# Transposes of an expert chunk three matmuls later, behind the wait for the next chunk's second weight unit

## The chip, the cores and the metric

The kernel runs on one core of one Trainium2 chip. The metric is device time in microseconds. Before the change the median of three runs is 1539.44 us (1539.42 to 1541.25).

## The reference

One step of a small hybrid decoder, for 256 prompt tokens and 32 sample tokens that share all weights: a convolution block, a dense SwiGLU, shared keys and values, windowed attention, and at the end a mixture of eight SwiGLU experts of which each token takes two. Everything is float32. The change lies in the mixture alone:

```python
h = rms_norm(x, g); hf = h.reshape(-1, D_MODEL)               # D_MODEL 1024
top_v, top_i = lax.top_k((hf @ w_router), TOP_K)              # 2 of 8
gates = jax.nn.softmax(top_v, axis=-1)
for e in range(N_EXPERTS):                                    # D_FF_EXPERT 3584
    he = jax.nn.silu(hf @ w_eg[e]) * (hf @ w_eu[e])
    y = y + combine[:, e:e + 1] * (he @ w_ed[e])
```

## The kernel before

Tokens are routed first: each of eight trips of the expert loop gathers the tokens of one expert into 128 slots. A trip walks through 14 chunks of 256 hidden columns. A chunk needs three weight units of 128 x 2048 float32 (1 MB each): two for gate and up together (each holds half of the 1024 input rows, four blocks of 512 columns), one for the down product.

Float32 products are made of three products of a shorter format. Each unit lands in one of six buffers (`land`). ScalarE casts it (`w_hi` or `d_hi`), VectorE subtracts the cast from the original (`w_lo` or `d_lo`), and TensorE runs three matmuls for each block of weights (`mm3`, lines 385 to 387): high by high, low by high, high by low. So a unit has twelve matmuls of 512 columns, and the down product twelve as well. The `w` pair has four buffers (two chunks), `d` has two.

The engines walk through a trip in orders written out by hand, with semaphores between them:

- TensorE, for chunk `ch`: `gate_up(ch+1, 0)`, the first unit of the next chunk; `turn(ch)`, two transposes of `he` of this chunk into bank 6; `gate_up(ch+1, 1)`, the second unit; `down(ch)`. A `gate_up` waits first for `split`, the count of finished `w_lo`. `turn` waits for `he_ready`, and `down` for `heT_ready` and `d_split`. In the last chunk of a trip, `gate_up` belongs to the next trip and stands in conditional blocks. Behind some chunks other work follows: matmuls that place the next trip's slots (line 744), transposes of the next trip's gathered tokens (line 738), and in the last trip sums that come back (line 770).
- ScalarE: `silu(ch)` when both units of the chunk are multiplied; the cast `d_hi` of chunk `ch+1`, which waits until `down(ch-1)` has freed its buffer; `heT_hi` (line 1189), which waits for the transposes; then both casts `w_hi` of chunk `ch+2` (line 1114).
- VectorE: `he` (line 1634), the product of SiLU and up half; `d_lo` of chunk `ch+1` (line 1628); in chunk 4 also the next trip's picks (`place`, line 1588); `heT_lo` (line 1660); then both `w_lo` of chunk `ch+2` (line 1527), each of which counts `split` up.
- SyncE issues the loads of the units in order, each when the buffer's last user, a `w_lo` or `d_lo`, is done.

Ahead of the loop stand the two units of the first chunk. The transposes use line 806.

Of the kernel before, what the change touches and what calls it, by code (L numbers as in the profile page):

```python
# [39 lines left out]
P = 128  # L40
# [17 lines left out]
NCH = FE // CH  # L58
# [55 lines left out]
def build(nc, io):  # L114
    with ExitStack() as ctx:
# [3 lines left out]
        def sem(name):  # L119
            return ctx.enter_context(nc.semaphore(name))  # L120

        bank = [ctx.enter_context(nc.psum_tensor(f"bank{i}", [P, 512], F32)) for i in range(8)]
# [79 lines left out]
        def c(name):  # L202
            return con[:, CON[name][0]:CON[name][1]]

        ident = c("ident")
# [50 lines left out]
        esilu_ready, he_ready, heT_done, heT_hi_ready, heT_ready = (  # L256
            sem(n) for n in ("esilu_ready", "he_ready", "heT_done", "heT_hi_ready", "heT_ready"))
# [124 lines left out]
        def _(pe):  # L382
            def mm3(out, w, x, start, stop):

                pe.matmul(out, w[0], x[0], start=start, stop=False)  # L385
                pe.matmul(out, w[0], x[1], start=False, stop=False)  # L386
                return pe.matmul(out, w[1], x[0], start=False, stop=stop)  # L387

            def wblock(n, i):
                a, b = i * P, (i + 1) * P  # L390
                return w_hi[n % RING][:, a:b], w_lo[n % RING][:, a:b]

            def H(k, a=0, b=T):
                return H_hi[:, k, a:b], H_lo[:, k, a:b]

            def G(k):
                return G_hi[:, k, :], G_lo[:, k, :]
# [49 lines left out]
            for j in range(KT_D):  # L447
# [3 lines left out]
                for half in range(2):  # L451
                    out = bank[2 * (j % 2) + half][:, 0:T]
                    for k in range(KT_D):
                        if j == 0 and half == 0:
                            wait_h(0, k)
                        last = mm3(out, wblock(U_PW1 + j, KT_D * half + k), H(k), k == 0, k == KT_D - 1)
# [11 lines left out]
            for k in by_end:  # L468
# [4 lines left out]
                last = pe.matmul(MEAN[:, 0:T], c("mean_d"), C[:, k, :], start=(k == by_end[0]), stop=(k == by_end[-1]))  # L473
# [4 lines left out]
            for d in range(KT_D):  # L478
# [4 lines left out]
                for k in range(KT_D):  # L483
                    if d == 0:
                        wait_h(1, k)
                    last = mm3(bank[d % 4][:, 0:T], wblock(n, KT_D * (d % 2) + k), H(k), k == 0, k == KT_D - 1)
                last.then_inc(pw2_done, 1)

            for half in range(2):
                for i in range(FH):  # L490
# [5 lines left out]
                    for part in range(2):  # L496
# [3 lines left out]
                        for k in range(KT_D):  # L500
                            if f == 0 and part == 0:
                                wait_h(2, k)
                            last = mm3(out, wblock(n, KT_D * part + k), G(k), k == 0, k == KT_D - 1)
# [3 lines left out]
                for d in range(KT_D):  # L507
                    if KT_D * half + d >= 2:
                        pe.wait_ge(x_ffn, KT_D * half + d - 1)
                    for i in range(FH):  # L510
# [6 lines left out]
                        last = mm3(bank[4 + d % 2][:, 0:T], wblock(n, blk), (A_hi[:, a, :], A_lo[:, a, :]),  # L517
                                   i == 0, i == FH - 1)
# [5 lines left out]
            for t in range(2):  # L524
                for k in range(KT_D):
                    if t == 0:
                        wait_h(3, k)
                    last = mm3(bank[t][:, 0:T], wblock(U_K, KT_D * t + k), H(k), k == 0, k == KT_D - 1)
# [13 lines left out]
            for i, (t0, nt) in enumerate(TT):  # L542
                for k in range(KT_D):
                    a = k * 256
                    last = mm3(bank[2 + i // 2][0:nt, 256 * (i % 2):256 * (i % 2) + 256],
                               H(k, t0, t0 + nt), (w_hi[U_V % RING][:, a:a + 256], w_lo[U_V % RING][:, a:a + 256]),
                               k == 0, k == KT_D - 1)
# [5 lines left out]
            for i, (t0, nt) in enumerate(TT):  # L553
                last = pe.matmul(bank[6][0:nt, i:i + 1], rr[:, t0:t0 + nt], c("mean_head")[:, 0:1], start=True, stop=True)
# [3 lines left out]
            for t in range(KT_D):  # L558
# [5 lines left out]
                for k in range(KT_D):  # L564
                    if t == 0:
                        wait_h(4, k)
                    last = mm3(bank[t % 4][:, 0:T], wblock(n, KT_D * (t % 2) + k), G(k),
                               k == 0, k == KT_D - 1)
# [135 lines left out]
            for d in range(KT_D):  # L704
# [4 lines left out]
                for k in range(KT_D):  # L709
                    last = mm3(bank[d % 4][:, 0:T], wblock(n, KT_D * (d % 2) + k), H(k), k == 0, k == KT_D - 1)  # L710
# [18 lines left out]
            for j in range(3):  # L729
                m = TT[j][1]  # L730
                last = pe.matmul(STAT[:, 64:64 + NE], c("ones")[0:m, :], sel[0:m, j, :], start=(j == 0), stop=(j == 2))
            last.then_inc(pos_done, 1)

            def gather(trip, h):

                pe.wait_ge(xt_ready, 16 * (trip + 1))
                for k in range(4):
                    last = pe.transpose(bank[4 + h][:, P * k:P * k + P], xt[:, (4 * h + k) * P:(4 * h + k + 1) * P], ident)  # L738
                last.then_inc(gathered, 1)

            def slot_rows(out):

                for j, (t0, nt) in enumerate(TT):
                    last = pe.matmul(out[:, 0:2], pick[0:nt, j, :], tok[0:nt, j, :],  # L744
                                     start=(j == 0), stop=(j == 2))
                last.then_inc(rows_placed, 1)

            def turn_picks():

                for j, (t0, nt) in enumerate(TT):  # L750
                    last = pe.transpose(bank[4][:, t0:t0 + nt], pick[0:nt, j, :], ident[0:nt, 0:nt])
                last.then_inc(PT_done, 1)
# [10 lines left out]
            def sums_back(k):  # L763

                if k == 0:
                    pe.wait_ge(y_loaded, 48)
                if k >= 2:
                    pe.wait_ge(y_added, k - 1)
                for i, (t0, nt) in enumerate(TT):
                    last = pe.transpose(bank[7 - 2 * (k % 2)][:, t0:t0 + nt], y_tok[i][0:nt, P * k:P * k + P],  # L770
                                        ident[0:nt, 0:nt])
                last.then_inc(y_done, 1)
# [10 lines left out]
                pe.matmul(out[:, 0:T], oe_hi[:, P * k:P * k + P], PT[:, :], start=True, stop=False)  # L783
                pe.matmul(out[:, 0:T], oe_lo[:, P * k:P * k + P], PT[:, :], start=False, stop=True).then_inc(y_done, 1)

            def gate_up(trip, ch, h):

                n = DENSE + 2 * ch + h
                pe.wait_ge(split, trip * (2 * NCH) + n + 1)
                for k in range(4):  # L790
                    kk = 4 * h + k
                    last = mm3(bank[ch % 2][:, :], (xe_hi[:, kk * P:kk * P + P], xe_lo[:, kk * P:kk * P + P]),
                               (w_hi[n % RING][:, 512 * k:512 * k + 512], w_lo[n % RING][:, 512 * k:512 * k + 512]),
                               kk == 0, kk == KT_D - 1)
                last.then_inc(used, 1)

            pe.sem_inc(oe_ready, 2)
            pe.wait_ge(xe_ready, 1)
            gate_up(0, 0, 0)
            pe.wait_ge(xe_ready, 2)  # L800
            gate_up(0, 0, 1)
            with pe.Fori(0, n_trips) as trip:
                def turn(ch):
                    pe.wait_ge(he_ready, trip * NCH + ch + 1)
                    for k in range(2):
                        last = pe.transpose(bank[6][:, P * k:P * k + P], he[:, P * k:P * k + P], ident)  # L806
                    last.then_inc(heT_done, 1)

                def down(ch):
                    pe.wait_ge(heT_ready, trip * NCH + ch + 1)  # L810
                    if ch == 0:
                        pe.wait_ge(oe_ready, trip * 2 + 2)
                    pe.wait_ge(d_split, trip * NCH + ch + 1 + 2)
                    for h in range(2):
                        for k in range(2):
                            a = D * k + 512 * h
                            last = mm3(bank[2 + h][:, :], (heT_hi[:, P * k:P * k + P], heT_lo[:, P * k:P * k + P]),
                                       (d_hi[ch % 2][:, a:a + 512], d_lo[ch % 2][:, a:a + 512]),
                                       ch == 0 and k == 0, ch == NCH - 1 and k == 1)
                    last.then_inc(d_used, 1)  # L820

                for ch in range(NCH):
                    if ch + 1 < NCH:
                        gate_up(trip, ch + 1, 0)
                        turn(ch)
                        gate_up(trip, ch + 1, 1)
                    else:

                        with pe.If(trip < n_trips - 1):
                            pe.wait_ge(xe_ready, trip * 2 + 3)  # L830
                            gate_up(trip, NCH, 0)
                        turn(ch)
                        with pe.If(trip < n_trips - 1):
                            pe.wait_ge(xe_ready, trip * 2 + 4)
                            gate_up(trip, NCH, 1)
                    down(ch)
                    if SUMS_AT <= ch < SUMS_AT + KT_D // 2:
                        with pe.If(trip > n_trips - 2):
                            sums_back(2 * (ch - SUMS_AT))
                            sums_back(2 * (ch - SUMS_AT) + 1)  # L840
                    if ch == PICKS_AT:
                        with pe.If(trip > n_trips - 2):
                            turn_picks()
                    if ch == GATHER_AT:
                        with pe.If(trip < n_trips - 1):
                            gather(trip + 1, 0)
                            gather(trip + 1, 1)
                    if ch == PLACE_AT + 2:
                        with pe.If(trip < n_trips - 1):
                            pe.wait_ge(P_ready, trip + 2)  # L850
                            slot_rows(bank[5])
# [1071 lines left out]
```

## Time and profile before

| | us |
|---|---|
| median of 3 runs | 1539.44 |
| the profiled execution | 1538.34 |
| its span, first to last instruction | 1536.5 |
| TensorE matmuls busy | 1502.2 (98%) |
| VectorE busy | 1225.9 (80%) |
| ScalarE busy | 967.6 (63%) |
| mean granted clock of TensorE | 0.984 |

Busy time of an engine is the union of its instructions. Weight loads of TensorE are listed apart (PEld) since they run beside matmuls. A matmul's duration in the trace goes beyond the start of the next one, so the distance between starts tells its cost. The expert stage lasts from about 560 us to the end.

### The profile page before, as it was taken

How to read it: one execution, taken by the hardware profiler on the slowest of the kernel's cores; microseconds unless marked ns; L12 is line 12 of the kernel's file. 1: busy time of each engine (PE TensorE's matmuls, PEld its weight loads, DVE VectorE, ACT ScalarE, POOL GpSimd, SP SyncE). 2: the span in 40 equal slices, each digit the busy share in tenths (PEclk: the TensorE clock that was granted, in tenths of full speed). 3: DMA queues.
4: the chain of work that ended last, by engine and by line, in shares of the span. 5: the costliest groups of instructions: out<-in, count | busy, mean ns of one | idle time of the engine just before them, and what ended most of it. 6: DMA issues, size and time to landing. Idle time of an engine off the chain costs nothing.

```text
span 1536.5 us, 21962 instructions
## 1 busy us (share of the span) xinstructions
PE 1502.2 (98%) x7841; PEld 1276.5 (83%) x7841; DVE 1225.9 (80%) x1259; ACT 967.6 (63%) x1068; POOL 117.4 (8%) x99
## 2 busy tenths in 40 slices
PE   8998999999999989999999999999999999999998
PEld 6997999999875978888888888888888888888776
DVE  6996545546696668898899889889889889889885
ACT  6654543344565357777677777777677777777764
POOL 2001011012320100000000000000000000000000
PEclk9999999999988989999999999999999999999999
DMA  9940345344531569989989989998998998998992
GB/s 352 168 141 28 110 165 178 138 151 165 192 114 63 195 237 370 377 306 413 396 310 404 404 339 369 404 373 335 407 385 320 422 375 312 423 387 300 416 367 105
DMA packets 66546, 438.47 MB, mean 285 GB/s; under 512 B 8101, under 2 KB 10405, under 8 KB 15936
## 3 DMA queue, kind: packets, MB, share of 16 engines
q1 hardware_dynamic: 57600, 412.38, 68.2%
q0 software_dynamic: 5552, 19.36, 5.2%
q10 hardware_dynamic: 3344, 6.05, 1.1%
q8 instruction: 33, 0.54, 0.1%
q14 instruction: 17, 0.14, 0.0%
HBM read 423.73 MB, written 15.03 MB: 286 GB/s over the span
## 4 chain that ended last, share of the span: by engine, by line
PE 90%; DVE 4%; ACT 2%; DMA 2%; issue 1%; POOL 1%; ACTq 0%; DVEq 0%; POOLq 0%; SPq 0%
PE bank L385 27%; PE bank L387 26%; PE bank L386 26%; PE bank L443 3%; PE bank L806 2%; DMA land<-in_w_expert 1%; ACT w_hi L873 1%; PE bank L653 1%; PE bank L738 0%; PE bank L410 0%; PE bank L627 0%; PE bank L744 0%; PE bank L605 0%; PE bank L642 0%; ACT sq L883 0%
## 5 line engine op out<-in xcount | busy, mean ns | idle before, releaser
L1527 DVE TENSOR_TENSOR w_lo<-land,w_hi 128x2048 fp32r<-128x2048 f32 x224 | 504.1, 2287 | 72.7 <-ACT w_hi L1114 71.4
L1114 ACT CAST w_hi<-land 128x2048 fp32r<-128x2048 f32 x224 | 418.6, 1912 | 7.3 <-DMA land<-in_w_expert 3.7
L385 PE MATMUL bank<-w_hi,xe_hi 128*128 128x512 f32 x896 | 361.3, 403 | 1.5 <-DVE xe_lo L1615 1.0
L387 PE MATMUL bank<-w_hi,xe_lo 128*128 128x512 f32 x896 | 350.9, 392 | 0.0
L386 PE MATMUL bank<-w_lo,xe_hi 128*128 128x512 f32 x896 | 350.3, 391 | 0.0
L1628 DVE TENSOR_TENSOR d_lo<-land,d_hi 128x2048 fp32r<-128x2048 f32 x112 | 256.7, 2292 | 42.4 <-ACT d_hi L1117 41.6
L1117 ACT CAST d_hi<-land 128x2048 fp32r<-128x2048 f32 x112 | 213.4, 1907 | 120.6 <-PE bank L387 111.7
L387 PEld LDWEIGHTS bank<-w_hi,xe_lo 128*128 128x128 f32 x896 | 168.2, 188 | 36.2
L385 PEld LDWEIGHTS bank<-w_hi,xe_hi 128*128 128x128 f32 x896 | 168.3, 188 | 35.0 <-DVE xe_lo L1615 1.2
L386 PEld LDWEIGHTS bank<-w_lo,xe_hi 128*128 128x128 f32 x896 | 168.8, 188 | 32.1
L385 PE MATMUL bank<-d_hi,heT_hi 128*128 128x512 f32 x448 | 177.6, 396 | 1.4 <-DVE heT_lo L1660 1.4
L387 PE MATMUL bank<-d_hi,heT_lo 128*128 128x512 f32 x448 | 177.0, 395 | 0.0
L386 PE MATMUL bank<-d_lo,heT_hi 128*128 128x512 f32 x448 | 176.4, 394 | 0.0
L1232 DVE TENSOR_TENSOR w_lo<-land,w_hi 128x2048 fp32r<-128x2048 f32 (+1 forms) x56 | 126.9, 2272 | 17.6 <-ACT w_hi L873 17.3
L385 PE MATMUL bank<-G_hi,w_hi 128*128 128x288 f32 x416 | 125.3, 301 | 2.1 <-DVE G_lo L1245 2.1
L386 PE MATMUL bank<-G_lo,w_hi 128*128 128x288 f32 x416 | 123.2, 296 | 0.0
L387 PE MATMUL bank<-G_hi,w_lo 128*128 128x288 f32 x416 | 122.8, 295 | 0.0
L873 ACT CAST w_hi<-land 128x2048 fp32r<-128x2048 f32 (+1 forms) x56 | 104.4, 1872 | 24.5 <-PE bank L387 23.9
L1189 ACT CAST heT_hi<-bank 128x256 fp32r<-128x256 f32 x112 | 41.7, 372 | 116.5 <-PE bank L806 115.7
L385 PEld LDWEIGHTS bank<-d_hi,heT_hi 128*128 128x128 f32 x448 | 84.1, 188 | 23.2 <-issue 3.6
L387 PEld LDWEIGHTS bank<-d_hi,heT_lo 128*128 128x128 f32 x448 | 84.1, 188 | 20.0
L386 PEld LDWEIGHTS bank<-d_lo,heT_hi 128*128 128x128 f32 x448 | 84.2, 188 | 19.3
(274 smaller groups left out, 2081.8 us busy)
## 6 DMA issues: line engine op xcount, KB each, us to landing
land<-in_w_expert SPq DMA_DIRECT2D x336, 1024.0 KB, 6.3
land<-in_w_dense SPq DMA_DIRECT2D x54, 1024.0 KB, 4.8
rel_rows<-rb POOLq DMA_DIRECT2D x1, 3072.0 KB, 36.6
bias<-rel_rows ACTq DMA_DIRECT2D x4, 512.0 KB, 5.7
y_rows<-zero_rows POOLq DMA_DIRECT2D x3, 512.0 KB, 11.9
X<-in_x SPq DMA_DIRECT2D x4, 288.0 KB, 6.0
out_y<-X SPq DMA_DIRECT2D x4, 288.0 KB, 3.3
Us<-in_state POOLq DMA_DIRECT2D x1, 1088.0 KB, 9.5
```

The costliest lines, as they stand in the source:

```text
L385: pe.matmul(out, w[0], x[0], start=start, stop=False)
L386: pe.matmul(out, w[0], x[1], start=False, stop=False)
L387: return pe.matmul(out, w[1], x[0], start=False, stop=stop)
L443: last = pe.matmul(bank[4 + m % 2][:, 0:SEQ], diag[:, g, w - taps[0], :], Up[:, PE_CHANNELS[m], w:w + SEQ], start=(w == 0), stop=(w == CW ...
L806: last = pe.transpose(bank[6][:, P * k:P * k + P], he[:, P * k:P * k + P], ident)
L873: act.copy(w_hi[n % RING][:, 0:cols], land[n % LAND][:, 0:cols]).then_inc(hi_done, 1)
L1114: act.copy(w_hi[n % RING][:], land[(DENSE + u) % LAND][:]).then_inc(hi_done, 1)
L1117: act.copy(d_hi[ch % 2][:], land[(DENSE + u) % LAND][:]).then_inc(d_hi_done, 1)
L1189: act.copy(heT_hi[:], bank[6][:, 0:CH]).then_inc(heT_hi_ready, 1)
L1232: dve.tensor_tensor(w_lo[n % RING][:, 0:cols], land[n % LAND][:, 0:cols], w_hi[n % RING][:, 0:cols].bitcast(F32), ALU.subtract).then_inc(s ...
L1527: dve.tensor_tensor(w_lo[n % RING][:], land[slot][:], w_hi[n % RING][:].bitcast(F32), ALU.subtract).then_inc(split, 1)
L1628: dve.tensor_tensor(d_lo[ch % 2][:], land[slot][:], d_hi[ch % 2][:].bitcast(F32), ALU.subtract).then_inc(d_split, 1)
```

## The change

The transposes of chunk `ch` leave their place between the two units of chunk `ch+1`. They now stand inside the second unit, after the first block's three matmuls, and so after that unit's wait for `split`. The last chunk of a trip keeps its order. `turn` moves out of the loop and takes the trip as an argument.

```diff
-            def gate_up(trip, ch, h):
+            def gate_up(trip, ch, h, turned=None):
 
                 n = DENSE + 2 * ch + h
                 pe.wait_ge(split, trip * (2 * NCH) + n + 1)
...
                                kk == 0, kk == KT_D - 1)
+                    if k == 0 and turned is not None:
+                        turn(trip, turned)
                 last.then_inc(used, 1)
+
+            def turn(trip, ch):
+
+                pe.wait_ge(he_ready, trip * NCH + ch + 1)
+                for k in range(2):
+                    last = pe.transpose(bank[6][:, P * k:P * k + P], he[:, P * k:P * k + P], ident)
+                last.then_inc(heT_done, 1)
...
                     if ch + 1 < NCH:
                         gate_up(trip, ch + 1, 0)
-                        turn(ch)
-                        gate_up(trip, ch + 1, 1)
+                        gate_up(trip, ch + 1, 1, turned=ch)
                     else:
...
-                        turn(ch)
+                        turn(trip, ch)
```

## Rows read from the trace of the kernel before

**Rows 1.** Busy us (instructions) of PE, PEld, DVE, ACT, POOL; clock; DMA share, GB/s

```profile
1000.00:1100.00 100.00, 100.00 (x453) 81.40 (x452) 89.21 (x69) 74.00 (x62) 3.18 (x1) 1.00 0.93 370
```

**Rows 2.** Waits, 600 to 1510 us: who, for whom: total us, times, longest

```profile
ACT heT_hi L1189 <- PE bank L806: 105.1, 97, 2.2
DVE w_lo L1527 <- ACT w_hi L1114: 61.9, 85, 1.4
...
ACT d_hi L1117 <- DMA land<-in_w_expert: 8.9, 7, 1.6
...
PEld bank L385 <- DVE w_lo L1527: 0.9, 1, 0.9
```

**Rows 3.** Timeline of a chunk: start us, length us, engine, line, names, count [idle before]

```profile
1001.71 0.38 PE L806 MATMUL bank<-con,he 128*128 128x128 f32 x2
...
1002.12 0.37 ACT L1189 CAST heT_hi<-bank 128x256 fp32r<-128x256 f32 x1 [1.05 <-PE bank L806]
...
1002.39 3.72 ACT L1114 CAST w_hi<-land 128x2048 fp32r<-128x2048 f32 x2
...
1004.34 4.49 DVE L1527 TENSOR_TENSOR w_lo<-land,w_hi 128x2048 fp32r<-128x2048 f32 x2 [0.61 <-ACT w_hi L1114]
...
1007.24 0.19 PEld L385 LDWEIGHTS bank<-w_hi,xe_hi 128*128 128x128 f32 x1
...
1008.16 0.39 PE L385 MATMUL bank<-w_hi,xe_hi 128*128 128x512 f32 x1
...
1008.75 0.41 DVE L1634 TENSOR_TENSOR he<-silu_g,bank 128x256 f32<-128x256 f32 x1
...
1009.61 2.29 DVE L1628 TENSOR_TENSOR d_lo<-land,d_hi 128x2048 fp32r<-128x2048 f32 x1 [0.44 <-ACT d_hi L1117]
...
1009.98 0.39 PE L387 MATMUL bank<-w_hi,xe_lo 128*128 128x512 f32 x1
1009.98 0.37 PEld L806 LDWEIGHTS bank<-con,he 128*128 128x128 f32 x2
1010.21 0.38 PE L806 MATMUL bank<-con,he 128*128 128x128 f32 x2
1010.32 0.19 PEld L385 LDWEIGHTS bank<-w_hi,xe_hi 128*128 128x128 f32 x1
...
1010.66 0.39 PE L386 MATMUL bank<-w_lo,xe_hi 128*128 128x512 f32 x1
...
1011.82 0.42 DVE L1660 TENSOR_TENSOR heT_lo<-bank,heT_hi 128x256 fp32r<-128x256 f32 x1
...
1012.95 0.19 PEld L385 LDWEIGHTS bank<-d_hi,heT_hi 128*128 128x128 f32 x1
```

**Rows 4.** Timeline in the last trip, around a weight load that waited for w_lo

```profile
1438.20 2.29 DVE L1527 TENSOR_TENSOR w_lo<-land,w_hi 128x2048 fp32r<-128x2048 f32 x1 [1.34 <-ACT w_hi L1114]
...
1439.66 0.39 PE L387 MATMUL bank<-d_hi,heT_lo 128*128 128x512 f32 x1
1440.55 0.19 PEld L385 LDWEIGHTS bank<-w_hi,xe_hi 128*128 128x128 f32 x1 [0.94 <-DVE w_lo L1527]
...
1440.88 0.39 PE L386 MATMUL bank<-w_lo,xe_hi 128*128 128x512 f32 x1
```

**Rows 5.** Timelines of DVE, PEld and PE around a chunk 4

```profile
1078.66 2.29 DVE L1628 TENSOR_TENSOR d_lo<-land,d_hi 128x2048 fp32r<-128x2048 f32 x1 [0.44 <-ACT d_hi L1117]
...
1082.12 0.19 PEld L385 LDWEIGHTS bank<-d_hi,heT_hi 128*128 128x128 f32 x1 [0.15 <-issue]
...
1082.00 0.39 PE L387 MATMUL bank<-w_hi,xe_lo 128*128 128x512 f32 x1
...
1082.46 0.39 PE L386 MATMUL bank<-d_lo,heT_hi 128*128 128x512 f32 x1
```

**Rows 6.** Chain that ended last, expert stage: start us, length us, instructions of extra work

```profile
618.48 0.65 PE bank L744 x6
...
661.85 0.87 PE bank L738 x8
...
1457.86 0.94 PE bank L770 x6
```

More of the change, by code:

```diff
@@ L802, in _ @@
             with pe.Fori(0, n_trips) as trip:
[L803 to L807, printed above, removed]
                 def down(ch):
```

## The prediction

> **What bounds the kernel now.** I read the busy time by stretch first: in the expert stage TensorE is busy 100.00 of 100 us at granted clock 1.00 (2.4 GHz), while VectorE has 89.21, ScalarE 74.00 and the DMA engines a share of 0.93 [rows 1]. The reader is to see that only TensorE is full, so a change here can gain only if TensorE itself does less or waits less. The waits of the stage come next [rows 2]: ScalarE waits 105.1 us for the transposes (97 times), VectorE 61.9 us for ScalarE's casts, but the weight loads of TensorE have waited 0.9 us, once, for `w_lo`. So TensorE waits for nobody, and what others wait for TensorE is idle time off the bound. Then one chunk in the timeline [rows 3]: transposes at 1001.71 and 1010.21, so a chunk lasts 8.50 us. The reader is to follow there the chain that runs from one turn to the next chunk but one: transposes 1001.71, `heT_hi` 1002.12, the two `w_hi` casts from 1002.39, the two `w_lo` subtractions from 1004.34, and the weight load at 1007.24 that opens that chunk's first unit.
>
> **What the change does to TensorE's own work.** Nothing is added or removed: 13 of the 14 turns of a trip, 104 in all, stand three matmuls later. At 1008.16 to 1009.98 eight matmuls start in 1.82 us, 0.2275 each [rows 3], so three are 0.68 us. A turn has a matmul of the same kind ahead of it and behind it in both orders, and between L387 at 1009.98 and the L386 behind the turn at 1010.66 lie 0.68 us where two matmuls alone take 0.455: 0.225 for a turn, in either place. Cost: 0; from both sides, rival D below has the gain, and a loss has no row that speaks for it.
>
> **The two waits.** The wait for the second unit's split now stands ahead of three matmuls and the turn. VectorE makes `he` only after both `w_lo` of the unit pair (1004.34 plus 4.49 is 1008.83, `he` from 1008.75 [rows 3]), so whenever the turn may go the split is long done. It was done 1.49 us before the load at 1010.32; now it is 0.68 later, and the load 0.34 earlier (1009.98, as no turn stands before it): 0.47 are left. Cost 0; if that cover went, the loss would be what exceeds it. The wait for `he` now holds, besides the transposes, the nine matmuls behind them: `he` ends at 1009.16, 0.82 before the load of the last matmul ahead of the turn would let the turn's own load go (1009.98), and both move by 0.68. Cost 0.
>
> **What is late next: the chain behind the turn.** ScalarE sat idle before `heT_hi` until the transposes came (1.05 us before each in this stage, [rows 2] in total), and its casts follow without a gap, so `heT_hi`, both `w_hi`, both `w_lo`, the SiLU and `he` all move by 0.68, and with each `w_lo` the release of a landing buffer, for which SyncE issues the next load. TensorE's demand for `w_lo` does not move, since its own order up to the next chunk's first unit holds the same matmuls. How much is there to spare? One `w_lo` alone takes 2.29 [rows 4], so the first ends at 1004.34 + 2.29 = 1006.63, and the load that needs it starts at 1007.24: 0.61. A load that did wait started 0.06 after its `w_lo` (1438.20 + 2.29 = 1440.49, load at 1440.55 [rows 4]). So 0.55 are spare, 0.68 are taken, and the load comes 0.13 late.
>
> A late load is not yet a late matmul, because every load starts with the matmul ahead of it. At 1082.12 one started 0.12 after that matmul (1082.00), and the second matmul behind it came at 1082.46, 0.46 after 1082.00, two plain steps of 0.23: nothing lost [rows 5]. At 1440.55 one was 0.89 late (1439.66), and the second matmul came at 1440.88, 1.22 after 1439.66 instead of 0.46: 0.76 lost [rows 4]. Both give a cover of 0.12 to 0.13. So 0.13 late costs 0.00 to 0.01; four roundings of a hundredth make it 0 to 0.03. I take 0.01, since the nearest row, 0.12 late, cost nothing. The other end is the whole 0.13.
>
> That bears on the weight load of a full array. The Trainium skill, "TensorE: Matmul & The Clock Gate", section "Part 3: Packing small matmuls — row/col tiling", says that a weight load overlaps matmuls in flight only where the row groups differ; here they are all 128*128. By that rule nothing would cover a late load. The rows above speak against it in this kernel: the loads run beside the matmul ahead of them, and 0.12 late cost nothing; what it would make of the time is rival B.
>
> How often: a trip has 14 chunks; the first units of chunks 2 to 13 are cast behind a moved turn. In two of these TensorE has other work just before (the slot matmuls, 0.65, and the gather's transposes, 0.87 [rows 6]), more than the 0.13 that is missing. That leaves 10 in each of seven trips. In the last trip there are no slot matmuls and no gather, but the returning sums (0.94 in each of four chunks [rows 6]), the turning of the picks and the one late landing of [rows 4] cover six of the twelve, so 6 remain: 76 in all. 76 x 0.01 = 0.8 us (0 to 2.3).
>
> **`heT_lo` and the down matmuls.** `heT_hi` 0.68 later ends at about 1011.67, before `heT_lo` at 1011.82, which waits not for it but for `d_lo` ahead of it on VectorE. `d_lo` starts at 1009.61 after 0.44 idle; `he` now ends at 1009.84 instead of 1009.16, so it can start at 1009.76 (VectorE's operations overlap by 0.08, as 1008.83 and 1008.75 show) and is 0.15 later, `heT_lo` too. It ends at 1012.39; the down load at 1012.95 has room. But in chunk 4 of a trip the next trip's picks stand between `d_lo` and `heT_lo`, and the load is 0.12 late already (1082.12, against 1082.00 [rows 5]): all its cover is used. `d_lo` at 1078.66 has the same 0.44 idle and moves by 0.16, so the load is 0.28 late and 0.16 are lost. Seven trips place a successor: 7 x 0.16 = 1.1 us (0 if the cover is larger than seen, 2.0 with none). The first unit behind it is then no longer late. Trip ends keep their old order (the last turn of a trip is not moved), and the chunk 13 subtractions there wait for casts that start from TensorE's own end, so 0.
>
> **Sum.** 0.8 + 1.1 = 1.9 us. The profiled execution took 1538.34 us (span 1536.5 and 1.84 around it), so 1540.2 by it; the median of the runs shown, 1539.44, is 1.1 above, so 1541.3.
>
> **Rivals.**
> A, the forecast: 1541.3, with its own range 1539.3 (nothing lost) to 1544 (both upper bounds, 2.3 + 2.0). No measurable change.
> B, slower: no part of a late load is covered when it waits for `w_lo` rather than for `heT_lo`. Place: the first load of each unit pair; it decides from the point where the moved chain exceeds the spare 0.55. Price 76 x 0.13 + 7 x 0.28 = 11.8, 1551.3. For it: no row has a `w_lo` wait of about 0.1 ahead of a long matmul. Against it: the 0.89 one lost only 0.76. Chance 0.12.
> C, slower: landing buffers are released 0.68 later, and loads land later where the queues are full. For it: DMA share 0.93, and ScalarE waited for landings 8.9 us in seven waits [rows 1, 2]. Against it: the casts that need them are 0.68 later as well. If each trip lost 0.68 once: 5.4 + 1.9, 1546.7. Chance 0.12.
> D, faster: the wait for the split, which now stands behind the transposes, costs TensorE time there. A turn takes 0.225, while two transposes of 128 columns, at a quarter of 0.2275 each, would be 0.114; 0.11 x 104 = 11.5 less, 1527.9. Against it: the load at 1010.32 starts 0.11 after the transposes at 1010.21, hence with the second of them, as every load starts with what is ahead of it; no wait shows. Chance 0.04.
> That the change does not do what it says is the plain part of A: the transposes' own wait cost 0.00 in this chunk, so there is nothing for it to hide.
>
> **How the numbers follow.** A 0.72, B 0.12, C 0.12, D 0.04. No change is within 0.2%, 3.1 us, about what a measurement of this kernel can tell. Same: 0.68 of A and 0.02 of C, 0.70. Slower: 0.03 of A, B, 0.10 of C, 0.25. Faster: 0.01 of A and D, 0.05. The range reaches from just below no change, 1538.5, through C to 1547.5; B and D stay outside.
>
> **What would show it.** Right: idle before `heT_hi` 1.73 instead of 1.05; no idle before `d_lo`; idle before the first `w_lo` some 1.1 instead of 0.6; some 76 waits of weight loads for `w_lo`, each a few hundredths above the usual gap plus 0.13; and turns still 8.50 to 8.51 us apart, but about 8.66 behind chunk 4 (8.50 + 0.16). Wrong: turns 8.6 apart in plain chunks (B), longer waits of ScalarE for landings with TensorE late behind them (C), or turns under 8.45 (D).

## The result, and the profile after

The changed kernel takes 1543.6 us (median of 22 runs, 1540.5 to 1545.7), the kernel before 1540.2 (22 runs, 1536.7 to 1542.1): a ratio of 1.0019, with a 95% interval of 1.0012 to 1.0025. That is 1.8 to 3.9 us more: a loss of about 0.2%, small, but clear of zero. The forecast was 1541.3, which is 1.9 above the median known then.

The page's busy times of the whole span; TensorE is at 98%:

```profile
span 1541.2 us, 21962 instructions
...
PE 1504.5 (98%) x7841; PEld 1272.3 (83%) x7841; DVE 1217.9 (79%) x1259; ACT 966.8 (63%) x1068; POOL 115.0 (7%) x99
```

The span is 4.7 us longer than before (1536.5), but single spans differ by more than the change does. So the expert stage is measured by itself, from the start of its first gate load to the start of its last down matmul. Two views by tile give its ends (count, shortest, median and longest in ns, first and last start):

```profile
L385 PEld LDWEIGHTS bank<-w_hi,xe_hi x896: 186/188/190, 555.6 to 1523.4; 128*128 128x128 f32 x180
```

```profile
L387 PE MATMUL bank<-d_hi,heT_lo x448: 388/398/404, 567.3 to 1531.2; 128*128 128x512 f32 x150
```

The same views of before:

```profile
L385 PEld LDWEIGHTS bank<-w_hi,xe_hi x896: 186/188/191, 553.2 to 1518.7; 128*128 128x128 f32 x180
```

```profile
L387 PE MATMUL bank<-d_hi,heT_lo x448: 390/395/405, 565.0 to 1526.5; 128*128 128x512 f32 x150
```

The stage lasts 1531.2 - 555.6 = 975.6 us, and before it lasted 1526.5 - 553.2 = 973.3: it is 2.3 longer, at a granted clock of 1.00 in both. The other 2.4 lie ahead of the stage, in work that the change doesn't touch; a second profile of the changed kernel, below, starts its stage at 553.0. All stages below are measured in this way (the expectations count to the end of the last matmul, 0.4 more in every kernel).

The stretch of [rows 1] after, in the same columns. TensorE is as full as before, so a busy share of 100 hides a loss of this size; the distances between starts, below, show it.

```profile
1000.00:1100.00 100.00, 100.00 (x450) 80.51 (x449) 89.05 (x68) 73.73 (x62) 3.17 (x1) 1.00 0.95 373
```

The waits of [rows 2] after, 600 to 1510 us:

```profile
ACT heT_hi L1191 <- PE bank L803: 172.9, 104, 2.9
DVE w_lo L1529 <- ACT w_hi L1116: 104.0, 98, 1.8
...
PEld bank L385 <- DVE w_lo L1529: 12.2, 65, 1.3
...
ACT d_hi L1119 <- DMA land<-in_w_expert: 4.1, 5, 1.3
...
ACT w_hi L1116 <- DMA land<-in_w_expert: 1.5, 2, 1.1
```

Three things are to be seen. ScalarE's wait for the transposes grew by 67.8 us: some 100 turns came 0.68 later. The weight loads, which waited once for `w_lo` before, now wait 65 times. ScalarE's waits for landings became fewer; `d_hi` waited 8.9 us in seven before, and `w_hi` 3.7 in six:

```profile
ACT w_hi L1114 <- DMA land<-in_w_expert: 3.7, 6, 1.8
```

One chunk of after, as in [rows 3]: the chain behind the turn.

```profile
1073.76 0.41 DVE L1636 TENSOR_TENSOR he<-silu_g,bank 128x256 f32<-128x256 f32 x1
...
1074.09 2.28 DVE L1630 TENSOR_TENSOR d_lo<-land,d_hi 128x2048 fp32r<-128x2048 f32 x1
...
1074.99 0.39 PE L387 MATMUL bank<-w_hi,xe_lo 128*128 128x512 f32 x1
...
1075.22 0.38 PE L803 MATMUL bank<-con,he 128*128 128x128 f32 x2
...
1075.64 0.37 ACT L1191 CAST heT_hi<-bank 128x256 fp32r<-128x256 f32 x1 [1.72 <-PE bank L803]
...
1075.67 0.39 PE L386 MATMUL bank<-w_lo,xe_hi 128*128 128x512 f32 x1
...
1075.91 3.72 ACT L1116 CAST w_hi<-land 128x2048 fp32r<-128x2048 f32 x2
...
1076.29 0.42 DVE L1662 TENSOR_TENSOR heT_lo<-bank,heT_hi 128x256 fp32r<-128x256 f32 x1
...
1077.86 4.49 DVE L1529 TENSOR_TENSOR w_lo<-land,w_hi 128x2048 fp32r<-128x2048 f32 x2 [1.15 <-ACT w_hi L1116]
```

From the transposes to the first `w_lo` it is 2.64 us, as before (1001.71 to 1004.34 was 2.63). The chain keeps its length and starts 0.68 later. The turn itself costs what it did: from the L387 ahead of it to the L386 behind it are 0.68 us (1074.99 to 1075.67), as before. Where the chain arrives late, another chunk shows, in the weight loads and then the matmuls:

```profile
993.99 0.19 PEld L385 LDWEIGHTS bank<-w_hi,xe_hi 128*128 128x128 f32 x1 [0.17 <-DVE w_lo L1529]
```

```profile
993.86 0.40 PE L387 MATMUL bank<-d_hi,heT_lo 128*128 128x512 f32 x1
994.10 0.39 PE L385 MATMUL bank<-w_hi,xe_hi 128*128 128x512 f32 x1
994.33 0.40 PE L386 MATMUL bank<-w_lo,xe_hi 128*128 128x512 f32 x1
...
995.02 0.39 PE L386 MATMUL bank<-w_lo,xe_hi 128*128 128x512 f32 x1
...
995.95 0.39 PE L387 MATMUL bank<-w_hi,xe_lo 128*128 128x512 f32 x1
```

The load at 993.99 starts 0.13 after the matmul at 993.86. The second matmul behind that one comes 0.47 after it, where 0.46 is usual. Then the eight steps from 994.10 to 995.95 take 1.85. Before, the same eight steps took 1.83:

```profile
1007.47 0.39 PE L385 MATMUL bank<-w_hi,xe_hi 128*128 128x512 f32 x1
...
1009.30 0.39 PE L387 MATMUL bank<-w_hi,xe_lo 128*128 128x512 f32 x1
```

So the late load itself costs about 0.005 us; the rest goes in the matmuls behind it, which follow each other a little more slowly. Plain chunks are those away from a trip's ends, from chunk 4 and from TensorE's other work: six in each of the first seven trips. Their time is counted from the first matmul of a chunk's first unit to that of the next chunk. Averaged over these 42, it went from 8.503 to 8.527 us: 0.024 more, nearly all of it between the last down matmul ahead of the unit and the unit's twelfth matmul.

Chunk 4, as in [rows 5], first the weight loads and then the matmuls:

```profile
1086.04 0.19 PEld L385 LDWEIGHTS bank<-d_hi,heT_hi 128*128 128x128 f32 x1 [0.27 <-issue]
```

```profile
1080.31 0.39 PE L385 MATMUL bank<-w_hi,xe_hi 128*128 128x512 f32 x1
...
1085.81 0.39 PE L387 MATMUL bank<-w_hi,xe_lo 128*128 128x512 f32 x1
1086.05 0.49 PE L385 MATMUL bank<-d_hi,heT_hi 128*128 128x512 f32 x1
1086.38 0.39 PE L386 MATMUL bank<-d_lo,heT_hi 128*128 128x512 f32 x1
...
1088.95 0.39 PE L385 MATMUL bank<-w_hi,xe_hi 128*128 128x512 f32 x1
```

The load is 0.23 late (0.12 before), and 1085.81 to 1086.38 is 0.57 instead of two steps of 0.23: 0.11 lost. From unit to unit this chunk takes 8.64 (1080.31 to 1088.95), against 8.51 for a chunk 4 before. It is the latest of the seven: in the other six trips the load is 0.22 late, the two steps lose 0.10, and the chunk takes 8.62.

### The profile page after: what moved, and what is told of

It reads as the page before. It is cut to its first block, busy times and chain, and to the rows that moved or that the text cites. A ratio compares the mean times of both kernels' runs of the same rounds, so it can differ in the third digit from the quotient of the medians.

```text
span 1541.2 us, 21962 instructions
## 1 busy us (share of the span) xinstructions
PE 1504.5 (98%) x7841; PEld 1272.3 (83%) x7841; DVE 1217.9 (79%) x1259; ACT 966.8 (63%) x1068; POOL 115.0 (7%) x99
## 4 chain that ended last, share of the span: by engine, by line
PE 90%; DVE 4%; ACT 2%; DMA 2%; issue 1%; POOL 1%; SPq 0%; ACTq 0%; DVEq 0%; POOLq 0%
PE bank L385 27%; PE bank L387 26%; PE bank L386 26%; PE bank L443 3%; PE bank L803 2%; DMA land<-in_w_expert 1%; ACT w_hi L875 1%; PE bank L653 1%; PE bank L738 0%; DMA X<-in_x 0%; DMA bias<-rel_rows 0%; PE bank L627 0%; PE bank L744 0%; PE bank L605 0%; PE bank L642 0%
## 5 line engine op out<-in xcount | busy, mean ns | idle before, releaser
L387 PE MATMUL bank<-w_hi,xe_lo 128*128 128x512 f32 x896 | 351.6, 392 | 0.0
L386 PE MATMUL bank<-w_lo,xe_hi 128*128 128x512 f32 x896 | 350.9, 392 | 0.0
L387 PEld LDWEIGHTS bank<-w_hi,xe_lo 128*128 128x128 f32 x896 | 168.2, 188 | 36.3
L386 PEld LDWEIGHTS bank<-w_lo,xe_hi 128*128 128x128 f32 x896 | 168.7, 188 | 29.8
L387 PE MATMUL bank<-d_hi,heT_lo 128*128 128x512 f32 x448 | 177.3, 396 | 0.0
L386 PE MATMUL bank<-d_lo,heT_hi 128*128 128x512 f32 x448 | 176.4, 394 | 0.0
L386 PE MATMUL bank<-G_lo,w_hi 128*128 128x288 f32 x416 | 123.0, 296 | 0.0
L387 PE MATMUL bank<-G_hi,w_lo 128*128 128x288 f32 x416 | 122.6, 295 | 0.0
L387 PEld LDWEIGHTS bank<-d_hi,heT_lo 128*128 128x128 f32 x448 | 84.0, 188 | 20.0
L386 PEld LDWEIGHTS bank<-d_lo,heT_hi 128*128 128x128 f32 x448 | 84.1, 188 | 19.4
```

## The experiments

Three theories are told apart. **Theory 1**, the forecast: the turn itself is free in either place, and the time goes where the chain behind it is longer than its spare. **Theory 2**: a turn inside a unit costs TensorE something by itself. **Theory 3**: the wait for the split, ahead of the turn, costs. The rivals B to D of the prediction are judged on the same runs. A chunk's time below is the median of the plain chunks.

**The wait alone.** The old order, with the second unit's wait put ahead of the turn:

```diff
                         gate_up(trip, ch + 1, 0)
+                        pe.wait_ge(split, trip * (2 * NCH) + DENSE + 2 * (ch + 1) + 2)
                         turn(ch)
                         gate_up(trip, ch + 1, 1)
```

> The turn stays where it was before; only the wait for the second unit's split is put ahead of it too. Theory 1: he implies that the split is done, so nothing is waited for and nothing moves: chunks 8.50 us, 1540.2 within 0.5. Theory 3 (the wait ahead of the turn is what costs): chunks 8.52 or more, 1542 to 1544.

Measured: 1540.15 us, ratio 1.0003 (0.9994 to 1.0012); stage 554.1 to 1527.2, 973.1; chunk 8.50. The loads wait as rarely as before:

```profile
PEld bank L385 <- DVE w_lo L1528: 0.9, 1, 0.9
```

Theory 3 falls: the wait ahead of the turn costs nothing. Rival D isn't settled by this run, since a wait still stands behind the transposes here. It is settled by the changed kernel and the next run, where none does: the turn takes the same 0.225 (above), and no chunk is shorter.

**The turn two matmuls into the unit.** Inside a unit too, but the chain moves by 0.455 instead of 0.68. The block's `mm3` is written out as its three matmuls (`xw` and `ws` are the high and low parts of its tokens and weights):

```diff
...
                     if k == 0 and turned is not None:
+                        pe.matmul(bank[ch % 2][:, :], xw[0], ws[0], start=False, stop=False)
+                        pe.matmul(bank[ch % 2][:, :], xw[0], ws[1], start=False, stop=False)
                         turn(trip, turned)
+                        last = pe.matmul(bank[ch % 2][:, :], xw[1], ws[0], start=False, stop=False)
...
```

> The turn stands behind two matmuls of the second unit instead of three, 0.455 us later than before instead of 0.68. Theory 1 (the chain from the turn over heT_hi, w_hi and w_lo to the first load of the next chunk but one runs out of its spare 0.55 us): 0.10 us are still spare, that load is not late, plain chunks last 8.50 us, chunk 4 at most 0.02 longer, and the expert stage is within 0.5 us of before: 1540.2, at most 1540.7. Theory 2 (a turn inside a unit costs TensorE time in itself): plain chunks 8.52 to 8.53 as with three matmuls, 1542.6 or more.

Measured: 1540.15 us, ratio 0.9993 (0.9984 to 1.0002); stage 973.1 (552.8 to 1525.9); chunk 8.50. From the waits of 600 to 1510 us:

```profile
ACT heT_hi L1195 <- PE bank L807: 150.8, 105, 2.7
...
PEld bank L385 <- DVE w_lo L1533: 1.0, 1, 1.0
```

ScalarE waits 45.7 us longer for the transposes than before, and still only one load waits, as before. Theory 2 falls: a turn inside a unit costs nothing while the chain stays within its spare, which therefore lies between 0.455 and 0.68, as the 0.55 of the prediction does.

**Four and six matmuls.** In the changed kernel the turn goes behind the first matmul of the unit's second block, or behind that whole block:

```diff
 four:
...
-                    if k == 0 and turned is not None:
+                    if k == 1 and turned is not None:
+                        pe.matmul(bank[ch % 2][:, :], xw[0], ws[0], start=False, stop=False)
                         turn(trip, turned)
+                        pe.matmul(bank[ch % 2][:, :], xw[0], ws[1], start=False, stop=False)
+                        last = pe.matmul(bank[ch % 2][:, :], xw[1], ws[0], start=False, stop=False)
...
 six:
-                    if k == 0 and turned is not None:
+                    if k == 1 and turned is not None:
                         turn(trip, turned)
```

> The turn stands behind four matmuls of the second unit, 0.91 us later than before. Theory 1: the first load is 0.36 late, 0.12 covered, 0.02 lost behind it: plain chunks 8.76, 76 x 0.26 = 20 us more, about 1560. Theory 2: 8.52 to 8.53, 1542.6 to 1544.

> The turn stands behind six matmuls of the second unit, 1.365 us later than before. Theory 1: the first load is 0.81 us late instead of 0.13, of which 0.12 is covered and some 0.02 are lost behind it: plain chunks last 9.2 us, 76 x 0.7 = 53 us more, about 1593. Theory 2 (a turn inside a unit costs in itself, wherever): 8.52 to 8.53, 1542.6 to 1544. Theory 4 (landings that come later are the cost): ScalarE's waits for landings grow with the shift.

Measured: four, 1556.75 us, ratio 1.0102 (1.0084 to 1.0121), stage 990.6, chunk 8.74; six, 1593.16 us, ratio 1.0343 (1.0324 to 1.0362), stage 1026.2, chunk 9.20. The waits of 600 to 1510 us, first four, then six:

```profile
PEld bank L385 <- DVE w_lo L1533: 27.5, 71, 0.8
```

```profile
PEld bank L385 <- DVE w_lo L1529: 59.6, 71, 0.9
...
PE bank L385 <- DVE w_lo L1529: 28.4, 71, 0.4
```

The forecast's own working gives both. Four moves the chain by 0.91: 0.91 - 0.55 - 0.12 = 0.24 per chunk, measured 0.24. Six moves it by 1.365: 0.69, measured 0.70. The expectation for four had added 0.02 for slower matmuls behind the load, and with 8.76 and 1560 came out too high. Past the cover a chunk loses what its chain is late. ScalarE's waits for landings don't grow with the shift (theory 4, the prediction's C): in the same stretch they make 1.9 us with four matmuls, and none is left with six. Theory 1 has its slope: 8.50, 8.53, 8.74 and 9.20 us for two, three, four and six matmuls.

**The chain alone.** The kernel before, its turn in the old place, with an idle copy on ScalarE between `heT_hi` and the casts (chunks 0 to 11), once of 736 columns and once of 640:

```diff
+DELAY = 736
 ...
                     act.copy(heT_hi[:], bank[6][:, 0:CH]).then_inc(heT_hi_ready, 1)
                     if ch + 2 < NCH:
+                        act.copy(idle_to[:], con[:, 0:DELAY])
+                    if ch + 2 < NCH:
                         expert_hi(trip, ch + 2, 0)
```

> The kernel before, its turn in the old place, with a copy of 128 x 736 on ScalarE between heT_hi and the first w_hi cast of chunks 0 to 11 (it writes a scratch tile that nothing reads). From 1.91 us for 2048 columns and 0.37 for 256 it should take 0.78, 0.68 more on the chain. Theory 1: first loads 0.12 to 0.13 late, plain chunks 8.52 to 8.53, chunk 4 8.6, the same 1542.5 to 1543.5 as the changed kernel. Theory 2 (the turn inside a unit costs): 1540.2, chunks 8.50.

> As the kernel with the copy on ScalarE, with 128 x 640, 0.60 us more on the chain. Theory 1: 0.55 are spare, so the load is 0.05 late, well inside the cover of 0.12, and plain chunks stay at 8.50 to 8.51; in chunk 4 the down load is 0.2 late and loses 0.08: 1540.2 to 1541. If a late load costs its lateness without cover: 76 x 0.05 = 4 us, 1544.

Measured: 736 columns, 1545.43 us, ratio 1.0031 (1.0019 to 1.0044), stage 977.4, chunk 8.54; 640 columns, 1542.84 us, ratio 1.0016 (1.0006 to 1.0027), stage 975.5, chunk 8.52. ScalarE's timeline with 736 columns shows the size of the delay:

```profile
1091.84 0.37 ACT L1190 CAST heT_hi<-bank 128x256 fp32r<-128x256 f32 x1 [1.05 <-PE bank L807]
1092.11 0.81 ACT L1192 CAST idle_to<-con 128x736 bf16<-128x736 f32 x1
1092.82 3.72 ACT L1115 CAST w_hi<-land 128x2048 fp32r<-128x2048 f32 x2
```

The casts start 0.71 later than without the copy (1092.82 instead of 1092.11), and `heT_hi` waits 1.05 as before: the turn hasn't moved. The loads come some 0.15 late, and the chunk loses 0.04. So the delayed chain alone does to the plain chunks what the change does, and a little more, since 0.71 is more than 0.68. The time is a miss (1542.5 to 1543.5 expected), and the stage's +4.1 shows why, counted over the first seven trips: 63 late units at 0.041 make 2.6, chunk 4's down load, 0.24 to 0.26 late, makes 0.8, and chunk 0's makes 0.6. The last isn't the chain's doing. There ScalarE sits idle for 0.82 to 1.03 us instead of 0.74 before its copy of the finished trip's output, which comes ahead of a cast `d_hi`, and the down load is 0.29 to 0.51 late instead of 0.23. It is so in both delayed kernels, and in the second version of the next experiment, which has no idle copy; why, no run here shows. A second side effect is small: `he` moves with the casts while the turn stays, so the turn's load, 0.81 behind `he` before, is mostly 0.15 behind it, and in eight chunks up to 0.10 late.

With 640 columns the delay is 0.63, and the time is again a miss (1540.2 to 1541 expected). The weight load and the matmuls of one chunk:

```profile
1069.02 0.19 PEld L386 LDWEIGHTS bank<-w_hi,xe_hi 128*128 128x128 f32 x1
```

```profile
1068.95 0.39 PE L388 MATMUL bank<-d_hi,heT_lo 128*128 128x512 f32 x1
1069.18 0.39 PE L386 MATMUL bank<-w_hi,xe_hi 128*128 128x512 f32 x1
1069.41 0.40 PE L387 MATMUL bank<-w_lo,xe_hi 128*128 128x512 f32 x1
```

The load is 0.07 late and the second matmul not at all, 0.46 behind the first; yet the chunk takes 0.01 to 0.02 longer. I had expected nothing to be lost inside the cover. In this kernel chunk 0's down load is 0.29 late or more (0.23 before) and chunk 4's some 0.19 (0.12). With these two, seven trips of 9 x 0.016 + 0.09 + 0.07 make 2.1, and the stage has +2.2. Both delays give the same spare for the chain: 0.71 - 0.15 and 0.63 - 0.07 are 0.56.

**The first cast ahead of the wait.** In the changed kernel, ScalarE casts the first `w_hi` before it waits for the transposes; in a second version not in chunks 2 to 4 of the last trip:

```diff
+                    if ch + 2 < NCH:
+                        expert_hi(trip, ch + 2, 0)
                     act.wait_ge(heT_done, trip * NCH + ch + 1)
                     act.wait_ge(d_used, trip * NCH + ch + 2)
                     act.copy(heT_hi[:], bank[6][:, 0:CH]).then_inc(heT_hi_ready, 1)
                     if ch + 2 < NCH:
-                        expert_hi(trip, ch + 2, 0)
                         expert_hi(trip, ch + 2, 1)
 second version, ahead of the wait (and the reverse behind it):
+                    if 2 <= ch <= 4:
+                        with act.If(trip < n_trips - 1):
+                            expert_hi(trip, ch + 2, 0)
+                    elif ch + 2 < NCH:
+                        expert_hi(trip, ch + 2, 0)
```

> The changed kernel, with ScalarE's first w_hi cast of chunk ch+2 ahead of heT_hi instead of behind it. Theory 1: the first w_lo no longer hangs on the turn but on heT_lo; the load of the first unit is over 1 us early, plain chunks are back at 8.50 us, chunk 4 loses nothing, and the time is 1539.5 to 1541. heT_hi comes up to 0.1 us later behind the cast, still ahead of the d_lo that heT_lo waits for; where a landing is tight (chunks 3 and 4) it can be held by up to 0.7 us, some 0.3 us of loss per trip at most. Theory 2 (a turn inside a unit costs in itself): plain chunks stay at 8.52 to 8.53, 1542.6 or more.

> The changed kernel with the first w_hi cast ahead of heT_hi, except in chunks 2 to 4 of the last trip, where it stays behind. Theory 1: trips 0 to 6 as with the cast always ahead (843.4 us from the stage's first unit to the last trip's), and the last trip without its late landing of 3.4 us, as in the changed kernel (130.5): 1540.2 to 1541. If the 2.5 us of the kernel with the cast always ahead were not those of its last trip: 1542.5 to 1543.

Measured, first version: 1543.02 us, ratio 1.0017 (1.0007 to 1.0026), stage 976.3; 1539.5 to 1541 was expected. The plain chunk is back at 8.50, no gate load is late, and the seven first trips take 843.4 us (before 843.2, changed kernel 845.5). But three chunks of the last trip lose what was won. ScalarE's timeline there, and VectorE's:

```profile
1436.45 1.90 ACT L1116 CAST w_hi<-land 128x2048 fp32r<-128x2048 f32 x1 [2.09 <-DMA land<-in_w_expert]
1438.25 0.36 ACT L1193 CAST heT_hi<-bank 128x256 fp32r<-128x256 f32 x1
```

```profile
1438.65 0.42 DVE L1663 TENSOR_TENSOR heT_lo<-bank,heT_hi 128x256 fp32r<-128x256 f32 x1 [1.97 <-ACT heT_hi L1193]
```

The cast now ahead of `heT_hi` waits 2.09 us for its weights, and `heT_lo`, which the down matmuls need, waits behind it. The second version keeps the cast behind in those chunks: 1540.92 us, ratio 1.0001 (0.9992 to 1.001), stage 974.2. Its waits:

```profile
ACT heT_hi L1196 <- PE bank L803: 25.7, 28, 1.7
...
PEld bank L385 <- DVE w_lo L1536: 1.7, 3, 1.4
```

With the turn where the change put it and the chain freed, the time is that of before. It isn't below it: of the stage's +0.9, about 0.7 is chunk 0's down load, 0.29 to 0.31 late in six trips and 0.51 in one, instead of 0.23, as in the delayed kernels. No version beat the kernel before.

**The changed kernel again, and chunk 4 by itself.** The second kernel puts the next trip's picks behind `heT_lo` instead of ahead of it:

```diff
-                    if ch == PLACE_AT:
-                        dve.wait_ge(y_free, trip + 1)
-                        ...
                     dve.wait_ge(heT_hi_ready, trip * NCH + ch + 1)
                     dve.tensor_tensor(heT_lo[:], ...).then_inc(heT_ready, 1)
+                    if ch == PLACE_AT:
+                        dve.wait_ge(y_free, trip + 1)
+                        ...
```

> The changed kernel once more, for a second profile. Theory 1: the expert stage, from its first unit's load to its last down matmul, takes 976.0 us again within 0.3 (before: 973.6), whatever the part ahead of it does; that part, 2.3 us later in the first profile, is not the change's and may fall anywhere between 552.8 and 556. Time 1542.5 to 1543.6. If the part ahead belonged to the change, it would end at 555 or later again.

> The changed kernel with the next trip's slot row copy and picks behind heT_lo of chunk 4 instead of ahead of it. Theory 1: the down load of chunk 4 is no longer 0.22 late, so its 0.10 go; the first load behind it, which that loss had covered, is then 0.13 late as elsewhere and loses 0.02 to 0.03. Seven trips x 0.07 = 0.5 us of the 2.4 go: stage 975.5, 1542 to 1543. If the picks were not what made that load late, chunk 4 stays at 8.61 and the stage at 976.0.

Measured: again, 1542.49 us, ratio 1.0017 (1.0008 to 1.0027), stage 975.9 (553.0 to 1528.9). So the stage's +2.3 repeats as +2.6, and the time ahead of it doesn't repeat. Picks behind: 1541.92 us, ratio 1.0008 (0.9998 to 1.0018), stage 975.1 (554.4 to 1529.5). VectorE's timeline around that chunk 4:

```profile
1083.31 0.42 DVE L1657 TENSOR_TENSOR heT_lo<-bank,heT_hi 128x256 fp32r<-128x256 f32 x1
1083.64 0.14 DVE L1661 COPY back_row<-slot_row 128x1 int32<-128x1 int32 x1
```

The down load behind it is no longer late; it starts with the last gate matmul ahead of it:

```profile
1084.33 0.19 PEld L385 LDWEIGHTS bank<-d_hi,heT_hi 128*128 128x128 f32 x1
```

```profile
1084.33 0.39 PE L387 MATMUL bank<-w_hi,xe_lo 128*128 128x512 f32 x1
```

The seven losses made 0.7, and the first seven trips give back 0.5 against either profile of the changed kernel: with TensorE no longer held up in chunk 4, the first load behind it is late again, ten in a trip instead of nine. By the times alone the two kernels can't be told apart; the stage and the load tell it.

## Why the prediction was right

- **The bound and the turn's own cost (0): right.** TensorE is busy 100.00 of 100 us in both kernels, and the turn in a unit costs nothing (0.68 for the turn and two steps in both places; two matmuls, 973.1).
- **The two waits (0): right** (973.1 with the split's wait alone ahead; in the changed kernel no load of a turn waits for `he`).
- **The chain, 0.13 late: right.** `heT_hi` idles 1.72 (1.73 forecast), `d_lo` nothing, the first `w_lo` 1.15 (some 1.1). The gate load is 0.12 to 0.13 late.
- **How often: nearly right.** Ten chunks of a trip were counted; nine visible waits in a trip were found. The tenth is the unit behind chunk 4, which the prediction itself called no longer late and then counted. In the last trip six loads are late, as counted, but that trip can't show their cost: its one long wait for a landing differs from profile to profile (the load 0.89 late before, 1.30 after), and the trip comes out 0.0 longer in one profile of the changed kernel and 0.3 in the other.
- **The cover: right at its edge, mis-sized behind it.** The second matmul is 0.005 late, where 0.01 was taken. But I looked only at the second matmul; the seven behind it give up another 0.02. So the term is 63 x 0.024 = 1.5, not 76 x 0.01 = 0.8; 0.024 is within the bound of 0.03.
- **Chunk 4: right in kind, 0.10 instead of 0.16.** The load came 0.22 to 0.24 late, not 0.28. From the last gate matmul to the second down matmul the chunk loses 0.10 in six trips and 0.11 in one; seven make 0.7, not 1.1.
- **Together** 2.2 against a forecast of 1.9; the stage has 2.3 and 2.6, the ratio 1.8 to 3.9. That the sum came so near is in part luck: the plain chunks were put 0.7 too low, by the slower spacing and in spite of too many events, and chunk 4 was put 0.4 too high.

B falls: three matmuls cost 0.024 and not 0.13 per chunk. C falls: ScalarE's waits for landings fell in sum from 8.9 and 3.7 (`d_hi`, `w_hi`) to 4.1 and 1.5, and with six matmuls there were none. D falls: without a wait behind the transposes a turn takes 0.225 as before.

On the weight loads: the Trainium skill, "TensorE: Matmul & The Clock Gate", section "Part 3: Packing small matmuls — row/col tiling", says that a weight load overlaps matmuls in flight only where the row groups differ; by that rule alone these full arrays would have had no cover. The runs don't agree: a load 0.13 late cost 0.005 at the next matmuls.

## What to carry to other kernels

An instruction pair that is free on the full engine can still be the head of a chain on idle ones: before moving it, subtract its move from the spare at the chain's end, and count where that end comes round again. Put a chain's first long step ahead of the wait only where that step's own input is sure to be there, or its wait becomes everyone's. Where the bound engine is full and waits for nobody, as here, making the others wait longer for it can at best change nothing.

## What was not expected of the hardware

A weight load that is late but still covered isn't quite free. With the load 0.12 to 0.13 late, the matmuls of 512 columns behind it follow each other at 0.231 to 0.232 us for eight steps in about half of the units, where from the fifth on 0.227 is usual (0.927 instead of 0.907 for four), and for fewer in most others (0.917 for those four). The unit loses 0.02 to 0.03 in all, and with the load only 0.07 late still 0.01 to 0.02. The trace of before had held it: there a down load 0.12 late left a chunk of 8.51 instead of 8.50. Why the spacing stays wide for so long, no run here shows.
